# Latent value products with high and low values side by side

## The chip, the cores and the metric

The kernel runs on one core of one Trainium2 chip. The metric is the device time in microseconds, the median of several runs. TensorE is called PE in the profile, VectorE is DVE, ScalarE is ACT, GpSimd is POOL, and SP is the engine that issues most transfers.

## The reference, cut to what matters

One encoder layer on 768 tokens (a prompt of 512 and a sample of 256): a layer norm, a combined projection, two kinds of attention in parallel (latent attention with 8 heads, differential attention with 4), an output projection, a second norm, and 16 experts of which each token uses two. All in f32. The part at hand is the latent attention:

```
def mla_attention(q_nope, q_rope, k_nope, k_rope, v):
    scale = (MLA_NOPE_DIM + MLA_ROPE_DIM) ** -0.5
    ...
        s = (einsum('bqhd,bkhd->bhqk', qn, k_nope) + einsum('bqhr,bkr->bhqk', qr, k_rope))
        p = softmax(s * scale, axis=-1)
        return einsum('bhqk,bkhd->bqhd', p, v)
```

A head has 64 value columns. The differential heads add the bias -slope x |q - k| to their scores; the slope of head h is 0.25 to the power h + 1, and the table in memory holds -|q - k|.

## The kernel before, in words

**Splitting.** Every f32 operand x of a matmul is kept as two tiles, high (x copied into the type fp32r by ScalarE, names in `_h`) and low (x minus high, by VectorE or GpSimd, names in `_l`). A product is three matmuls: high x high, low x high, high x low; `three` makes the list and `products` (L647) issues it.

**The latent stage** runs as 48 slots s = 6h + i (8 heads, 6 query tiles of 128 each: four of the prompt with 512 keys, two of the sample with 256). Each engine goes through its own `mla_slot(s)` in order, and semaphores join them. In slot s:
- PE turns the probabilities of tile s (`turn_probs`, L782, into bank 2 or 3), computes pieces of block projections B (the differential q and k), the scores of tile s+4, at i = 4, 5 the value product of the head's prompt unit w = 2h, at i = 1 that of the last head's sample unit w = 2h-1, and at the end of a slot fills for the head two further on: K at i = 2, 3, Q at i = 4, 5, values V at `V_SLOTS`.
- ACT copies the turned probabilities (`probs_high`), takes exp of tile s+3, and copies fills (`high`). DVE does maximum, reciprocal, `probs_low`, `low`. POOL scales the probabilities of tile s+2 (`normalise`) and makes low parts of q and weights.

**Banks.** Fills go through banks 4 and 5 (`bank_order`), several in turn: bank 5 takes K, K, Q, Q, B of a head. `begin(g)` makes PE wait until the one before was copied high and low (or, for Q, multiplied into `q_raw` by `q_rotated`). In the slots the copies of a fill stand one slot after it.

**The value product.** `product(w)` has a stationary operand of 128 value columns, two heads side by side, of which the 64 rows of its own head are used, and the turned probabilities moving (512 or 256 columns). It accumulates in bank 6. `mix_high` copies the 64 rows to `mixM_h` and `mix_low` makes `mixM_l` from the bank and that copy; the next unit's product waits for `mix_low` (`m_ml`).

**The hand-over.** From s = 45 the slots z = s - 49 of the differential stage run along: `diff_scores(z+4)` on PE, `diff_biased(z+3)` on DVE (score plus bias table, and its maximum), `diff_exp(z+3)` on ACT in two halves, `diff_reciprocals(z+2)`, `diff_second(z+2)` on POOL, `diff_probs(z+1)` on DVE, `diff_turn_probs(z)` (L854) on PE, and the output of z-1 with `dpT_h`, `dpT_l`. Output projection pieces (`o_part`) begin at z = 3 and need four weight tiles split by `wo_high` on ACT (at z = -2 to 1) and `wo_low` on DVE (z = -1 to 2). The bias table is multiplied by 0.25 ahead of each head, by the first too (L1497). The first two `diff_output` wait for all of `mixM_l`.

Behind it come the output projection, router and experts; the experts' weights are fetched by transfers that wait for the router's results and for buffers.

Of the kernel before, what the change touches and what calls it, by code (L numbers as in the profile page):

```python
# [27 lines left out]
P = 128  # L28
# [32 lines left out]
def encoder_trunk(nc, x_prompt, x_sample, ln0_g, ln0_b, w_in, g_q, g_kv, w_uq, w_ukv, lam_q1, lam_k1,  # L61
# [88 lines left out]
    v_h = [at(f"v_h{i}", (132, 18)[i], [P, NT, 4 * VDIM], FR) for i in range(2)]  # L150
    v_l = [at(f"v_l{i}", (144, 24)[i], [P, NT, 4 * VDIM], FR) for i in range(2)]
# [4 lines left out]
    mixM_h = at("mixM_h", 126, [P, HEADS // 2, TOK], FR)  # L156
    mixM_l = at("mixM_l", 138, [P, HEADS // 2, TOK], FR)
# [168 lines left out]
    def filled(g):  # L326
# [4 lines left out]
        if g[0] == "V":  # L331
            vs = slice(2 * g[2], 2 * g[2] + 2)
            return bank[:].rearrange("p (t n) -> p t n", t=2), v_h[g[1]][:, vs, :], v_l[g[1]][:, vs, :]
# [37 lines left out]
    for k in range(0, 4, 2):  # L371
        z = 3 + 3 * (k // 2)
        O_EARLY[z], O_LATE[z], O_ADDS_FIRST[z + 1] = ((k, 0, 6),), ((k, 6, 12),), k
        O_LATE[z + 1], O_EARLY[z + 2], O_ADDS_LAST[z + 2] = ((k + 1, 0, 6),), ((k + 1, 6, 12),), k + 1
    WO_SLOTS = {15: 0, 16: 1, 17: 2, 21: 3}
# [134 lines left out]
    def mix_parts(n, c):  # L510
        return ((mixM_h, mixM_l), (mixD_h, mixD_l))[n][0][:, c, :], ((mixM_h, mixM_l), (mixD_h, mixD_l))[n][1][:, c, :]
# [120 lines left out]
    def front_pe(pe):  # L632
# [152 lines left out]
        def product(w, js):  # L785
# [3 lines left out]
            if js[0] == 0:  # L789
# [4 lines left out]
                wait(pe, m_ml, w)  # L794
            vs = slice((h % 4) // 2 * P, (h % 4) // 2 * P + P)
            pairs = three([(v_h[h // 4][:, t, vs], v_l[h // 4][:, t, vs], pT_h[x][:, j, :], pT_l[x][:, j, :])
                           for j, t in enumerate(range(SEQS[x][0] // P, SEQS[x][0] // P + nk))])

            last = products(psum[6][:, 0:n], pairs, 3 * js[0], 3 * js[-1] + 3)
# [9 lines left out]
        def mla_slot(s):  # L809
# [8 lines left out]
            if i == 1 and h:  # L818
                product(2 * h - 1, (0, 1))
# [37 lines left out]
        def diff_output(g):  # L857
# [5 lines left out]
            if g < 2:  # L863
                pe.wait_ge(m_ml, 2 * HEADS)
                pe.wait_ge(m_ptl, MT)
# [8 lines left out]
        def o_part(k, first, end):  # L874
# [4 lines left out]
            if first == 0:  # L879
                if n == 0:  # L880
                    pe.wait_ge(m_ml, 2 * HEADS if t >= NT_P else 2 * HEADS - 1)
# [98 lines left out]
    def front_act(act):  # L980
# [93 lines left out]

        def mix_high(w):
# [3 lines left out]
            act.wait_ge(m_pv, w + 1)  # L1079
            nc.scalar.activation(mixM_h[r, h // 2, t0:t0 + n], psum[6][r, 0:n], ACT.Copy).then_inc(m_mh, 1)  # L1080
# [10 lines left out]
        def mla_slot(s):  # L1091
            h, i = s // NT, s % NT
            if s < MT:
                probs_high(s)
            if i == 0 and h:
                mix_high(2 * h - 2)
            if i == 2 and h:
                mix_high(2 * h - 1)
            if s + 3 < MT:
                exp(s + 3)  # L1100
            if s >= MT:
# [1424 lines left out]
```

## Time and profile before

| | us |
|---|---|
| median of 3 runs | 803.47 (803.02 to 804.69) |
| the profiled execution, its time | 802.8 |
| its span, first to last instruction | 801.0 |
| PE busy in the span | 739.7 |
| mean granted TensorE clock | 0.98 of full |

The profile gives for each engine the time in which it was busy, the waits with what ended them, and a timeline with the start and duration of each instruction. Matmuls overlap: the duration of one is longer than the distance to the next, so their cost is read from the distances between starts. The granted clock is 1.00 at 2.4 GHz and 0.50 at 1.2 GHz. The latent slots run from about 110 to 276 us, the differential stage to about 390 us, the experts from about 455 us.

### The profile page before, as it was taken

What the parts mean: (1) busy time and instruction counts of PE and PEld (TensorE: products, weight loads), DVE (VectorE), ACT (ScalarE), POOL (GpSimd) and SP (SyncE); (2) the same over time, 40 slices, a digit from 0 to 9 for tenths busy, and PEclk for the clock granted to TensorE, in tenths of its full rate; (3) what the DMA queues carried; (4) which work ended last, traced back from release to release, by engine and by line L of the source; (5) the groups of instructions that cost most, each with busy time, mean ns of one, the idle gap of its engine ahead of it and who ended that gap; (6) DMA issues with size and microseconds to landing.
All of it is one profiled execution on the core that took longest, in us unless ns stands there. A gap on an engine that the chain in (4) does not pass through costs nothing.

```text
span 801.0 us, 12711 instructions
## 1 busy us (share of the span) xinstructions
PE 739.7 (92%) x3844; PEld 609.6 (76%) x3844; DVE 584.3 (73%) x975; ACT 482.5 (60%) x874; POOL 269.2 (34%) x292
## 2 busy tenths in 40 slices
PE   3999989998899889999999799999999999999985
PEld 3898878777778667777789577888877777777862
DVE  6964354555555586777678879999988888888857
ACT  3334355545554565667125447888788788888635
POOL 3132356545655243234421114222223222322111
PEclk9999999999999959999999999999999999999998
DMA  9724320222025492132645759999999999999863
GB/s 344 247 97 132 118 74 7 80 66 66 0 68 182 159 367 84 35 119 79 220 180 208 261 165 363 390 380 388 392 383 375 378 373 365 391 378 377 298 210 158
DMA packets 71485, 179.37 MB, mean 224 GB/s; under 512 B 11687, under 2 KB 28071, under 8 KB 71444
## 3 DMA queue, kind: packets, MB, share of 16 engines
q1 hardware_dynamic: 66692, 166.34, 55.2%
q0 software_dynamic: 4752, 12.51, 6.2%
q8 instruction: 23, 0.38, 0.2%
q14 instruction: 18, 0.15, 0.1%
HBM read 153.20 MB, written 30.42 MB: 229 GB/s over the span
## 4 chain that ended last, share of the span: by engine, by line
PE 55%; DMA 19%; DVE 14%; ACT 6%; issue 4%; POOL 1%; SPq 1%; ACTq 0%; DVEq 0%; POOLq 0%
PE bank L647 31%; DMA rawG<-in_w_gate 16%; PE bank L1767 4%; PE bank L1769 3%; PE bank L1768 3%; PE bank L782 2%; DVE eGl L1922 2%; DMA dv_l<-dv_low 2%; PE bank L1790 1%; PE bank L1789 1%; PE bank L1788 1%; ACT eGh L1852 1%; DVE eUl L1922 1%; PE bank L2147 1%; DVE eDl L1922 1%
## 5 line engine op out<-in xcount | busy, mean ns | idle before, releaser
L1922 DVE TENSOR_TENSOR eDl<-rawD,eDh 128x1024 fp32r<-128x1024 f32 x68 | 80.2, 1221 | 12.4 <-ACT eDh L1852 12.2
L1266 POOL TENSOR_SCALAR me<-me,mrec 128x512 f32<-128x512 f32 (+1 forms) x48 | 64.9, 1355 | 55.5 <-DVE mrec L1445 55.5
L1922 DVE TENSOR_TENSOR eGl<-rawG,eGh 128x1024 fp32r<-128x1024 f32 x64 | 75.5, 1222 | 7.5 <-ACT eGh L1852 6.6
L1922 DVE TENSOR_TENSOR eUl<-rawU,eUh 128x1024 fp32r<-128x1024 f32 x68 | 78.8, 1220 | 2.5 <-ACT eUh L1852 2.5
L2045 POOL DMA_INDIRECT acc_rows<-yg,idx_s x16 | 29.7, 1859 | 134.6 <-ACT yg L1877 134.6
L1852 ACT ACTIVATE eGh<-rawG 128x1024 fp32r<-128x1024 f32 x64 | 65.7, 1058 | 7.7 <-DMA rawG<-in_w_gate 7.2
L1072 ACT ACTIVATE pT_h<-bank 128x512 fp32r<-128x512 f32 (+1 forms) x48 | 25.3, 527 | 73.9 <-PE bank L782 73.9
L1451 DVE TENSOR_TENSOR pT_l<-bank,pT_h 128x512 fp32r<-128x512 f32 (+1 forms) x48 | 28.9, 602 | 50.3 <-ACT pT_h L1072 50.3
L1767 PE MATMUL bank<-eGh,xgT_h 128*128 128x512 f32 x136 | 56.5, 416 | 8.6 <-DVE xgT_l L1927 7.5
L1852 ACT ACTIVATE eDh<-rawD 128x1024 fp32r<-128x1024 f32 x64 | 64.0, 1055 | 0.0
L1852 ACT ACTIVATE eUh<-rawU 128x1024 fp32r<-128x1024 f32 x64 | 62.8, 1052 | 0.0
L1767 PE MATMUL bank<-eUh,xgT_h 128*128 128x512 f32 x136 | 54.6, 401 | 0.0
L1769 PE MATMUL bank<-eGl,xgT_h 128*128 128x512 f32 x136 | 53.8, 396 | 0.0
L1768 PE MATMUL bank<-eGh,xgT_l 128*128 128x512 f32 x136 | 53.4, 393 | 0.0
L1769 PE MATMUL bank<-eUl,xgT_h 128*128 128x512 f32 x136 | 53.2, 391 | 0.0
L1768 PE MATMUL bank<-eUh,xgT_l 128*128 128x512 f32 x136 | 52.9, 389 | 0.0
L1790 PE MATMUL bank<-eDl,hT_h 128*128 128x512 f32 x128 | 49.9, 390 | 0.0
L1788 PE MATMUL bank<-eDh,hT_h 128*128 128x512 f32 x128 | 49.8, 389 | 0.0
L1789 PE MATMUL bank<-eDh,hT_l 128*128 128x512 f32 x128 | 49.8, 389 | 0.0
L647 PE MATMUL bank<-xT_h,wb_h 128*128 128x256 f32 (+1 forms) x128 | 44.9, 351 | 4.0 <-DVE q_raw L1432 2.4
L647 PE MATMUL bank<-xT_h,wb_l 128*128 128x256 f32 (+1 forms) x128 | 43.7, 342 | 0.0
L647 PE MATMUL bank<-xT_l,wb_h 128*128 128x256 f32 (+1 forms) x128 | 43.7, 341 | 0.0
(345 smaller groups left out, 2171.6 us busy)
## 6 DMA issues: line engine op xcount, KB each, us to landing
rawG<-in_w_gate SPq DMA_DIRECT2D x68, 512.0 KB, 15.6
rawU<-in_w_up SPq DMA_DIRECT2D x68, 512.0 KB, 12.3
rawD<-in_w_down SPq DMA_DIRECT2D x68, 512.0 KB, 13.6
wb_raw<-in_w_in SPq DMA_DIRECT2D x8, 512.0 KB, 4.5
wo_raw<-in_w_o SPq DMA_DIRECT2D x8, 512.0 KB, 7.4
xln_rows<-res SPq DMA_DIRECT2D x6, 512.0 KB, 3.9
dqk_high<-st_h SPq DMA_DIRECT2D x8, 384.0 KB, 2.3
dqk_low<-st_l SPq DMA_DIRECT2D x8, 384.0 KB, 3.3
```

The source lines that it names most:

```text
L647: last = nc.tensor.matmul(out, pairs[i][0], pairs[i][1], start=(i == 0), stop=(i == n - 1))
L1266: nc.gpsimd.tensor_scalar(e, e, mrec[:, g % NSB:g % NSB + 1], None, ALU.mult).then_inc(m_p, 1)
L1451: nc.vector.tensor_tensor(pT_l[x][:, :, qs], psum[2 + g % 2][:, 0:n].rearrange("p (j q) -> p j q", q=P), f32(pT_h[x][:, :, qs]), ALU.subtr ...
L1767: nc.tensor.matmul(out, xgT_h[:, c, :], wh_[X][i][:, cs], start=(c == 0), stop=False)
L1768: nc.tensor.matmul(out, xgT_l[:, c, :], wh_[X][i][:, cs], start=False, stop=False)
L1769: last = nc.tensor.matmul(out, xgT_h[:, c, :], wl_[X][i][:, cs], start=False, stop=(c == KD - 1))
L1788: nc.tensor.matmul(out, hT_h[:, cs], wh_["D"][c][:, ns], start=(c == 0), stop=False)
L1789: nc.tensor.matmul(out, hT_l[:, cs], wh_["D"][c][:, ns], start=False, stop=False)
L1790: last = nc.tensor.matmul(out, hT_h[:, cs], wl_["D"][c][:, ns], start=False, stop=(c == 3))
L1852: nc.scalar.activation(wh_[X][i][:], raw_of(X, t, i)[:], ACT.Copy).then_inc(s_hi[X], 1)
L1922: nc.vector.tensor_tensor(wl_[X][i][:], raw_of(X, t, i)[:], f32(wh_[X][i][:]), ALU.subtract).then_inc(s_lo[X], 1)
L2045: pool.indirect_dma_start(out=acc_rows, out_offset=bass.IndirectOffsetOnAxis(ap=idx_s[:, 0:1], axis=0), in_=yg[:], in_offset=None, bounds_ ...
```

## The change

- The values are stored per head as 128 columns, 64 high and 64 low (`v_hl`). A product is now two matmuls per key tile, that stationary operand with the high and with the low probabilities; the rows of the bank hold the high values' part in one half and the low values' part in the other.
- The two halves are summed: ACT copies one half across partitions to `mixM_sum` (`mix_moved`), DVE adds the other (`mix_summed`), and then `mix_high` and `mix_low` split the sum, both operands now in SBUF. The next product waits for the sum alone. The order of these in each engine's slots is new.
- The copies of filled banks stand in the slot of the fill: B at i = 0, 1, K at 2, 3, V at its slot; `q_rotated(h+1, 1)` is ahead of `probs_low`.
- The hand-over: the last product moves from slot 49 to 48, `mix_moved(14)` to slot 47, the first reciprocals and probabilities of the differential stage and the wo copies to other slots (`WO_FIRST`), and the bias table comes multiplied by 0.25, so the first head's multiply is dropped.

```
```diff
@@ -147,14 +147,14 @@
     st_l = at("st_l", 121, [P, TOK], FR)
-    v_h = [at(f"v_h{i}", (132, 18)[i], [P, NT, 4 * VDIM], FR) for i in range(2)]
-    v_l = [at(f"v_l{i}", (144, 24)[i], [P, NT, 4 * VDIM], FR) for i in range(2)]
+    v_hl = [at(f"v_hl{i}", (138, 18)[i], [P, NT, 4, 2 * VDIM], FR) for i in range(2)]
...
     me = [at(f"me{i}", 198 + 2 * i, [P, 512]) for i in range(NME)]
-    mixM_h = at("mixM_h", 126, [P, HEADS // 2, TOK], FR)
-    mixM_l = at("mixM_l", 138, [P, HEADS // 2, TOK], FR)
+    mixM_h = [at(f"mixM_h{c}", 126 + 12 * (c // 2) + 3 * (c % 2), [P, TOK], FR) for c in range(HEADS // 2)]
+    mixM_sum = [at(f"mixM_sum{c}", 132 + 12 * (c // 2) + 3 * (c % 2), [P, TOK]) for c in range(HEADS // 2)]
+    mixM_l = [at(f"mixM_l{c}", 132 + 12 * (c // 2) + 3 * (c % 2), [P, TOK], FR) for c in range(HEADS // 2)]
@@ -330,7 +330,8 @@
             vs = slice(2 * g[2], 2 * g[2] + 2)
-            return bank[:].rearrange("p (t n) -> p t n", t=2), v_h[g[1]][:, vs, :], v_l[g[1]][:, vs, :]
+            v = v_hl[g[1]][:, vs, :, :]
+            return bank[:].rearrange("p (t h n) -> p t h n", t=2, h=4), v[:, :, :, 0:VDIM], v[:, :, :, VDIM:2 * VDIM]
@@ -372,6 +373,7 @@
         O_LATE[z + 1], O_EARLY[z + 2], O_ADDS_LAST[z + 2] = ((k + 1, 0, 6),), ((k + 1, 6, 12),), k + 1
+    WO_FIRST = {-1: (0,), 0: (1,), 1: (2, 3)}
@@ -508,7 +510,7 @@
     def mix_parts(n, c):
-        return ((mixM_h, mixM_l), (mixD_h, mixD_l))[n][0][:, c, :], ((mixM_h, mixM_l), (mixD_h, mixD_l))[n][1][:, c, :]
+        return (mixM_h[c][:], mixM_l[c][:]) if n == 0 else (mixD_h[:, c, :], mixD_l[:, c, :])
...
     def front_sync(sp):
         def load_x(t):
@@ -791,12 +793,13 @@
-                wait(pe, m_ml, w)
-            vs = slice((h % 4) // 2 * P, (h % 4) // 2 * P + P)
-            pairs = three([(v_h[h // 4][:, t, vs], v_l[h // 4][:, t, vs], pT_h[x][:, j, :], pT_l[x][:, j, :])
-                           for j, t in enumerate(range(SEQS[x][0] // P, SEQS[x][0] // P + nk))])
-            last = products(psum[6][:, 0:n], pairs, 3 * js[0], 3 * js[-1] + 3)
+                wait(pe, m_ml, 2 * w - 1)
+            pairs = []
+            for j, t in enumerate(range(SEQS[x][0] // P, SEQS[x][0] // P + nk)):
+                v = v_hl[h // 4][:, t, h % 4, :]
+                pairs += [(v, pT_h[x][:, j, :]), (v, pT_l[x][:, j, :])]
+            last = products(psum[6][:, 0:n], pairs, 2 * js[0], 2 * js[-1] + 2)
@@ -815,7 +818,7 @@
                 product(2 * h, ((0, 1), (2, 3))[i - 4])
-            if i == 1 and h:
+            if i == (1 if s < MT else 0) and h:
@@ -861,7 +864,7 @@
             if g < 2:
-                pe.wait_ge(m_ml, 2 * HEADS)
+                pe.wait_ge(m_ml, 4 * HEADS)
@@ -878,7 +881,7 @@
                 if n == 0:
-                    pe.wait_ge(m_ml, 2 * HEADS if t >= NT_P else 2 * HEADS - 1)
+                    pe.wait_ge(m_ml, 4 * HEADS if t >= NT_P else 4 * HEADS - 2)
@@ -1072,12 +1075,19 @@
+        def mix_moved(w):
+            h, x = w // 2, w % 2
+            t0, n, _ = SEQS[x]
+            r, other = (slice(VDIM * i, VDIM * i + VDIM) for i in (h % 2, 1 - h % 2))
+            act.wait_ge(m_pv, w + 1)
+            nc.scalar.activation(mixM_sum[h // 2][r, t0:t0 + n], psum[6][other, 0:n], ACT.Copy).then_inc(m_mh, 1)
         def mix_high(w):
...
             r = slice(VDIM * (h % 2), VDIM * (h % 2) + VDIM)
-            act.wait_ge(m_pv, w + 1)
-            nc.scalar.activation(mixM_h[r, h // 2, t0:t0 + n], psum[6][r, 0:n], ACT.Copy).then_inc(m_mh, 1)
+            act.wait_ge(m_ml, 2 * w + 1)
+            nc.scalar.activation(mixM_h[h // 2][r, t0:t0 + n], mixM_sum[h // 2][r, t0:t0 + n], ACT.Copy).then_inc(m_mh, 1)
...
         def wo_high(n, c):
@@ -1090,26 +1100,31 @@
         def mla_slot(s):
             h, i = s // NT, s % NT
+            if s > MT:
+                return
...
                 probs_high(s)
-            if i == 0 and h:
-                mix_high(2 * h - 2)
-            if i == 2 and h:
-                mix_high(2 * h - 1)
+            w = {0: 2 * h - 2, 2: 2 * h - 1}.get(i, -1) if s < MT - 1 else {MT - 1: 2 * HEADS - 2, MT: 2 * HEADS - 1}[s]
+            if s == MT:
+                mix_high(2 * HEADS - 2)
+            if w >= 0:
+                mix_moved(w)
...
                 exp(s + 3)
+            if 0 <= w < 2 * HEADS - 2:
+                mix_high(w)
...
                 q_high(h + 1, 1)
-            if i in (1, 2) and h - 1 in BLOCK_OF:
-                high(("B", BLOCK_OF[h - 1], i - 1))
-            if i in (3, 4) and h + 2 < HEADS:
-                high(("K", h + 2, i - 3))
+            if i in (0, 1) and h - 1 in BLOCK_OF:
+                high(("B", BLOCK_OF[h - 1], i))
+            if s in V_SLOTS:
+                high(("V", 1, V_SLOTS[s]))
+            if i in (2, 3) and h + 2 < HEADS:
+                high(("K", h + 2, i - 2))
...
                 q_high(h + 2, 0)
-            if s - 1 in V_SLOTS:
-                high(("V", 1, V_SLOTS[s - 1]))
@@ -1159,8 +1174,10 @@
                 diff_exp(z + 3, 1)
-            if -2 <= z < 2:
-                wo_high(0, z + 2)
+            if z == -1:
+                mix_high(2 * HEADS - 1)
+            for c in WO_FIRST.get(z, ()):
+                wo_high(0, c)
@@ -1451,13 +1468,21 @@
+        def mix_summed(w):
+            h, x = w // 2, w % 2
+            t0, n, _ = SEQS[x]
+            r = slice(VDIM * (h % 2), VDIM * (h % 2) + VDIM)
+            total = mixM_sum[h // 2][r, t0:t0 + n]
+            dve.wait_ge(m_mh, 2 * w + 1)
+            nc.vector.tensor_tensor(total, total, psum[6][r, 0:n], ALU.add).then_inc(m_ml, 1)
         def mix_low(w):
...
             r = slice(VDIM * (h % 2), VDIM * (h % 2) + VDIM)
-            dve.wait_ge(m_mh, w + 1)
-            nc.vector.tensor_tensor(mixM_l[r, h // 2, t0:t0 + n], psum[6][r, 0:n], f32(mixM_h[r, h // 2, t0:t0 + n]),
-                                    ALU.subtract).then_inc(m_ml, 1)
+            dve.wait_ge(m_mh, 2 * w + 2)
+            nc.vector.tensor_tensor(mixM_l[h // 2][r, t0:t0 + n], mixM_sum[h // 2][r, t0:t0 + n],
+                                    f32(mixM_h[h // 2][r, t0:t0 + n]), ALU.subtract).then_inc(m_ml, 1)
...
         def mla_slot(s):
@@ -1467,22 +1492,29 @@
                 q_rotated(h + 2, 0)
+            if i == 0 and 1 <= h < HEADS - 1:
+                q_rotated(h + 1, 1)
...
                 probs_low(s)
-            if i == 0 and h:
-                mix_low(2 * h - 2)
-            if i == 2 and h:
-                mix_low(2 * h - 1)
+            if s == MT - 1:
+                diff_reciprocals(0)
+            w = {0: 2 * h - 2, 2: 2 * h - 1}.get(i, -1) if s < MT - 1 else {MT - 1: 2 * HEADS - 2, MT: 2 * HEADS - 1}.get(s, -1)
+            if s == MT:
+                mix_low(2 * HEADS - 2)
+            if w >= 0:
+                mix_summed(w)
+            if s < MT and i in (1, 3) and h:
+                mix_low(2 * h - 2 + i // 2)
+            if s == MT + 1:
+                mix_low(2 * HEADS - 1)
...
                 return
-            if i == 0 and 1 <= h < HEADS - 1:
-                q_rotated(h + 1, 1)
-            if i in (1, 2) and h - 1 in BLOCK_OF:
-                low(("B", BLOCK_OF[h - 1], i - 1))
-            if i in (3, 4) and h + 2 < HEADS:
-                low(("K", h + 2, i - 3))
-            if s - 1 in V_SLOTS:
-                low(("V", 1, V_SLOTS[s - 1]))
+            if i in (0, 1) and h - 1 in BLOCK_OF:
+                low(("B", BLOCK_OF[h - 1], i))
+            if s in V_SLOTS:
+                low(("V", 1, V_SLOTS[s]))
+            if i in (2, 3) and h + 2 < HEADS:
+                low(("K", h + 2, i - 2))
...
         def wo_low(n, c):
@@ -1493,9 +1525,10 @@
                     dve.wait_ge(s_const, CONSTS + 16)
-                wait(dve, s_bias, 2 * g)
-                nc.vector.tensor_scalar_mul(bias_t[:], bias_t[:], 0.25).then_inc(s_in, 1)
-                dve.wait_ge(s_in, h + 1)
+                else:
+                    dve.wait_ge(s_bias, 2 * g)
+                    nc.vector.tensor_scalar_mul(bias_t[:], bias_t[:], 0.25).then_inc(s_in, 1)
+                    dve.wait_ge(s_in, h)
@@ -1544,18 +1577,21 @@
                 diff_mix_low(z - 3)
+            if z == -1:
+                diff_reciprocals(1)
+                diff_probs(0)
...
                 diff_biased(z + 3)
-            if 0 <= z + 1 < DT:
+            if 0 <= z and z + 1 < DT:
...
                 diff_probs_low(z)
-            if 0 <= z + 2 < DT:
+            if 0 <= z and z + 2 < DT:
...
                 o_first(O_ADDS_LAST[z])
-            if -1 <= z < 3:
-                wo_low(0, z + 1)
+            for c in WO_FIRST.get(z - 1, ()):
+                wo_low(0, c)
@@ -2486,7 +2522,7 @@
     rope_table = np.stack([np.concatenate([plain, turned]), np.concatenate([turned, plain])]).astype(np.float32)
-    dist = -np.abs(np.arange(P)[:, None] - (np.arange(ALIBI_W)[None, :] - (SEQ_P - P))).astype(np.float32)
+    dist = -0.25 * np.abs(np.arange(P)[:, None] - (np.arange(ALIBI_W)[None, :] - (SEQ_P - P))).astype(np.float32)
```

## Rows read from the trace of the kernel before

**Rows 1.** The page's busy table: us, share of the span, instructions.
```profile
PE 739.7 (92%) x3844; PEld 609.6 (76%) x3844; DVE 584.3 (73%) x975; ACT 482.5 (60%) x874; POOL 269.2 (34%) x292
```

**Rows 2.** Windows of 10 us: busy per engine, then granted clock, DMA share, GB/s.
```profile
150.00:160.00 10.00, 9.37 (x61) 8.32 (x60) 4.73 (x10) 5.51 (x13) 8.18 (x6) 1.00 0.09 29
...
190.00:200.00 10.00, 9.57 (x45) 8.06 (x46) 5.07 (x12) 4.82 (x11) 6.58 (x4) 0.83 0.12 37
...
280.00:290.00 10.00, 6.92 (x35) 5.54 (x35) 9.94 (x24) 8.88 (x20) 4.34 (x3) 0.51 1.03 366
290.00:300.00 10.00, 10.00 (x53) 8.53 (x53) 6.60 (x18) 5.05 (x17) 3.74 (x7) 0.64 0.94 380
```

**Rows 3.** The chain that ended last, by line, as the page has it.
```profile
PE bank L647 31%; DMA rawG<-in_w_gate 16%; PE bank L1767 4%; PE bank L1769 3%; PE bank L1768 3%; PE bank L782 2%; DVE eGl L1922 2%; DMA dv_l<-dv_low 2%; PE bank L1790 1%; PE bank L1789 1%; PE bank L1788 1%; ACT eGh L1852 1%; DVE eUl L1922 1%; PE bank L2147 1%; DVE eDl L1922 1%
```

**Rows 4.** Timeline of PE, value products of 512 and 256 columns: start, duration.
```profile
151.67 0.40 PE L647 MATMUL bank<-pT_h,v_l 128*128 128x512 f32 x1
151.90 0.39 PE L647 MATMUL bank<-pT_l,v_h 128*128 128x512 f32 x1
...
158.70 0.28 PE L647 MATMUL bank<-pT_h,v_l 128*128 128x256 f32 x1
158.82 0.28 PE L647 MATMUL bank<-pT_l,v_h 128*128 128x256 f32 x1
```

**Rows 5.** Waits in 105 to 400 us, PE's: total us, times, longest.
```profile
PE bank L647 <- DVE mixM_l L1459: 2.7, 2, 2.4
PE bank L647 <- DVE k_l L1422: 2.6, 3, 2.1
...
PE bank L647 <- DVE q_raw L1432: 2.4, 5, 0.6
...
PE bank L647 <- DVE v_l L1422: 1.6, 1, 1.6
...
PE bank L647 <- DVE st_l L1420: 0.8, 1, 0.8
```

**Rows 6.** Timeline of PE behind the wait for k_l that ended at 190.43.
```profile
192.05 0.63 PE L647 MATMUL bank<-pT_h,v_h 128*128 128x512 f32 x1
192.48 0.63 PE L647 MATMUL bank<-pT_h,v_l 128*128 128x512 f32 x1
```

**Rows 7.** Groups by form, 105 to 300 us: busy us, mean ns, idle before.
```profile
L1504 DVE CUSTOM_DVE_ANT_0 ee<-bank,bias_t 128x512 f32<-128x512 f32 x10 | 6.5, 688 | 0.1
L1459 DVE TENSOR_TENSOR mixM_l<-bank,mixM_h 64x512 fp32r<-64x512 f32 x8 | 5.5, 683 | 2.6 <-ACT mixM_h L1080 2.5
...
L1121 ACT ACTIVATE ee<-ee,negmax 128x512 f32<-128x512 f32 x10 | 7.1, 715 | 5.0 <-DVE negmax L1504 5.0
L1080 ACT ACTIVATE mixM_h<-bank 64x512 fp32r<-64x512 f32 x8 | 4.7, 588 | 0.1
```

**Rows 8.** Timeline of the hand-over, PE, then ACT.
```profile
274.54 0.40 PE L647 MATMUL bank<-pT_l,v_h 128*128 128x512 f32 x1
...
279.54 0.36 PE L647 MATMUL bank<-pT_h,v_h 128*128 128x256 f32 x1 [2.36 <-DVE mixM_l L1459]
...
281.46 1.12 PE L854 MATMUL bank<-ident,pp 128*128 128x128 f32 x4 [0.84 <-DVE pp L1517]
...
285.23 1.08 PE L854 MATMUL bank<-ident,pp 128*128 128x128 f32 x4 [1.72 <-DVE dpT_l L1523]
286.84 0.45 PE L647 MATMUL bank<-dv_h,dpT_h 128*128 128x128 f32 x1 [0.52 <-issue]
...
277.01 1.04 ACT L1089 ACTIVATE wo_h<-wo_raw 128x1024 fp32r<-128x1024 f32 x1
278.08 0.59 ACT L1080 ACTIVATE mixM_h<-bank 64x512 fp32r<-64x512 f32 x1
```

**Rows 9.** Timeline of POOL, `diff_second` beside an idle and a busy DVE.
```profile
276.35 0.78 POOL L1287 TENSOR_SCALAR ee<-ee,erec,lam_col 128x512 f32<-128x512 f32 x1 [5.46 <-DVE erec L1510]
281.58 1.66 POOL L1287 TENSOR_SCALAR ee<-ee,erec,lam_col 128x512 f32<-128x512 f32 x1 [4.46 <-DVE erec L1510]
```

## The prediction

> **What bounds the kernel now.** I read the page's busy table first: TensorE is busy 92% of the span and no other engine comes near [rows 1]. That is an average over stages, so next the windows of 10 us. In the latent-attention stage (110 to 270 us) a typical window has PE at 9.4 of 10 us with VectorE at 4.7, ScalarE at 5.5 and hardly any DMA [rows 2]. The chain of the page names the matmuls of `products` (L647) first and the gate-weight transfer second [rows 3]. The transfers of the experts are issued behind events that the front produces (logits, stored rows, low parts), so the expert stage moves as one piece when the front ends sooner; I found no transfer that runs on a date of its own. What is saved in the front is therefore saved at the end. The change touches only the latent stage and the hand-over to the differential heads, so all below is read there.
>
> **Part 1, two products for three.** `product` issued 3 matmuls per key tile, 12 of 512 columns and 6 of 256 columns per head; now 8 and 4. Removed in 8 heads: 32 of 512 columns and 16 of 256. What one costs is the distance between starts, not the duration (0.39 and 0.28 us, overlapped): 151.90 - 151.67 = 0.23 us and 158.82 - 158.70 = 0.12 us [rows 4]. 32 x 0.23 + 16 x 0.12 = 7.4 + 1.9 = 9.3 us. TensorE sets the pace there, so this lies on the path, but for what the hand-over takes back (part 4).
>
> The Trainium skill (TensorE: Matmul & The Clock Gate, Back-to-back issue gap) gives about 131 ns per matmul for a sustained stream of load and matmul pairs at 512 columns; by it the 32 long ones would be worth 4.2 us instead of 7.4, and the forecast would be 3 us later. The trace has 0.23 us for just such pairs [rows 4], and I go by the trace.
>
> **Part 2, the added copies.** Each of 16 units gets `mix_moved` on ScalarE and `mix_summed` on VectorE. The nearest rows are the old `mixM_h` (0.59 us for 64x512) and `mixM_l` (0.68) [rows 7]; with the 256-column halves at about two thirds, that adds some 8 us to each engine over 160 us. Those engines are half idle [rows 2], so the busy time is hidden under the matmuls. What matters is bank 6, which the next unit's first product waits for: before, high then low; now moved then summed, the same two operations. `mix_high` and `mix_low` come later, from SBUF. `mix_high(w)` stands behind `exp(s+3)` (0.7 us and its accumulator read), which covers the sum it waits for. Queued behind it are `q_high(h+1,1)`, then POOL's `q_low`; I put them where they are now. Bounds: 0 if covered, 16 x 0.6 = 10 us if every copy sat on the path; I take 0, since the idle time of both engines is nearest.
>
> One row gives pause: `diff_second`, an SBUF operation of POOL, took 0.78 us while VectorE was idle and 1.66 us while it ran operations with two SBUF inputs [rows 9]. `mix_low` now reads two SBUF tiles where it read a bank. At worst VectorE or POOL is held about 0.9 us in each of 16 slots; POOL works two slots ahead, so I count nothing, and keep this for the rival below. The Trainium skill (SBUF — State Buffer, SBUF: two separate sides) says that a VectorE operation with two SBUF inputs and a GpSimd one that reads SBUF exclude each other for a whole instruction; the two rows agree. By it and the 0.9 us of the rows, 16 low parts that each stood on the path would take 14 us back and leave the time near 801, which is rival D by another way.
>
> **Part 3, fills copied in their own slot.** `high`/`low` of B go from slots 1, 2 to 0, 1, of K from 3, 4 to 2, 3, of V one slot sooner; `q_rotated(h+1,1)` goes ahead of `probs_low`. They free the banks for which TensorE stood. The waits of PE there [rows 5], each with 0.15 us for the refilled pipeline:
> - q_raw, 5 times, 2.4 + 0.8 = 3.2 us. The block piece at the end of slot 0 waits for it; now it is issued before `probs_low`, held only by POOL's `q_low`, which ends a microsecond before PE arrives. Gone.
> - k_l, 3 times, 2.6 + 0.5 = 3.1 us, gone. The longest, 2.1 us, was followed by a fall of the clock: 192.48 - 192.05 = 0.43 us a matmul where 0.23 is usual [rows 6], and the window shows 0.83 [rows 2]. Seven matmuls x 0.2 = 1.4 us, gone too.
> - v_l, 1.6 + 0.15; the chain still has two copies, so I count half, 0.8 us.
> - st_l (L1420), 0.8 + 0.15 us, gone; its sister L1422 waits mostly ahead of the slots, and I count 0.2 of it: 1.2 us together.
> - mixM_l, 2.7 in two: 2.4 belongs to the hand-over, 0.3 stays.
> Sum 3.2 + 3.1 + 1.4 + 0.8 + 1.2 = 9.7 us. But ScalarE now stands at the end of a slot for the fill, in order, ahead of `probs_high` of the next slot, and slots are 1.2 us a head shorter; a K fill is followed at once by K's second half in the same bank. I take 2 us for new waits: net 8. Ends: 0 (every wait forms again elsewhere) and 10.
>
> **Part 4, the hand-over.** I went through the four queues by hand on the clock of the trace of before, with the durations of [rows 7]: a half of exp 0.72 and some 0.2 for the read of its sum, a half of biased 0.69 less a small overlap, copies and low parts 0.59 and 0.68. Before, TensorE stood until 279.54 for `mix_low(14)`, because `wo_high` at 277.01 was ahead of `mix_high(14)` at 278.08 on ScalarE; `diff_turn_probs` ran at 281.46 and 285.23 [rows 8]. Now `product(14)`, last issued at 274.54, is over 0.9 us sooner; moved 273.9 to 274.5, summed to 275.2, `product(15)` at 275.3, its stall of 2.4 us gone. The bias multiply, which stood ahead of the first biased scores, is gone too and lets the first exp start some 0.6 us sooner. But what is late next: `biased(1)` comes behind the sum (to 276.3), exp(1) to 277.6, `mix_high(14)` to 278.1, and VectorE's `mix_low(14)` waits for that with `mix_summed(15)`, `diff_reciprocals(1)` and `diff_probs(0)` queued behind it. `diff_turn_probs(0)` comes to 280.0, so PE is idle some 2.6 us from 277.3; `mix_high(15)` behind exp(2) ends 282.7, and the second turn comes to 285.6. From there PE is the bound at a halved clock: the windows 280 to 300 show 0.51 and 0.64 [rows 2]. First output about 286.5 by my schedule, 286.84 before: 0.35 us sooner, of the 0.9 that two products had saved. So the hand-over gains nothing and costs 0.6 us of part 1. Bounds: +3 us (one more gap like the one I drew) if `mix_high` runs a slot later, and -7 if the gap closes and the clock holds: the two windows hold 2 x (0.49 + 0.36) x 10 = 17 us at half clock, with PE 0.85 busy, and half of that is 7. Moving the wo copies later is covered by TensorE's own work at half clock: they are needed at z = 3 only. Without that cover one more wo copy, about as long as two copies of [rows 7], would be late.
>
> **Sum.** -9.3 + 0.6 - 8.0 = -16.7. Against the profiled execution: 802.8 us (span 801.0 and 1.8 around it) gives 786; against the median 803.5, 787. The two differ by 0.1%; I use the median.
>
> **Rivals.**
> - A, as above: 787 (782 to 792). Chance 0.55.
> - B, only the matmuls: the freed banks come sooner, but ScalarE's ordered waits and the two-input copies make as many new stalls. For: ScalarE waits for PE at nearly every slot; against: 9.4 of 10 busy already, and each stall of part 3 has one named cause. 803.5 - 9.3 + 0.6 = 795 (792 to 799). Chance 0.20.
> - C, the hand-over clears as well (the mechanism of its lower bound): 787 - 7 = 780. For: the half clock came after stalls at 279 to 285. Against: my schedule has as long a gap. Chance 0.12.
> - D, no change: the 8 us added to ScalarE and VectorE lie on the path and take back what the matmuls give: 803.5 - 9.3 + 8 = 802 (it would show as PE waits on the new copies). Against: half idle engines. Chance 0.05.
> - E, slower: the gap after 277.3 drops the clock and the loose start of the differential heads (turns at 280.0 and 285.6 waiting for copies) keeps it down. A microsecond of full PE at half clock costs half a microsecond, so it has to stay down 2 x 16.7 = 33 us longer than the 17 us of before to undo the gain; 40 us longer gives 806.5. Against: before, it was back inside the second window. Chance 0.08.
> The range goes from C into B: 778 to 798. A measurement of this kernel tells about 0.2% (1.6 us) from no change. Faster: A, B, C and some of D, 0.88; same 0.04; slower 0.08.
>
> **What the changed profile would show.** Products at the same 0.23 and 0.12 us, 64 of 512 and 32 of 256 columns. PE's waits for q_raw, k_l, st_l in 120 to 260 us near nothing, and the granted clock 1.00 at 185 to 200. In the hand-over, PE waiting for pp (behind mixM_l) for 2 to 3 us instead of for mixM_l, the clock low for some 17 us after it, and the first output about 16 to 17 us earlier than 286.84, near 270. After 300 us each stage as long as before. I am wrong if new waits on ScalarE's copies stand in PE's list with more than 3 us, or if the hand-over differs by more than 3 us from my schedule.

## The result, and the profile after

The changed kernel takes 797.86 us (median of 4 runs, 796.42 to 800.24) against 803.96 (803.02 to 804.69) for the kernel before on the same chip: 6.1 us less, ratio 0.9923, 95% interval 0.9897 to 0.9948. I had forecast 787. The sign was right, the size was not. The profiled execution has a span of 798.4 us, 2.6 under the 801.0 of before. The ratios here and below leave out executions in a slower state of the chip and are estimated from the single runs, so that they differ by up to 0.4% from the quotient of two medians.

**The matmuls did go away.** The timeline of PE in the changed kernel shows the value products at the distances forecast, two of each key tile, next to [rows 4]: 150.45 - 150.22 = 0.23 us and 157.02 - 156.91 = 0.11 us.

```profile
150.22 0.39 PE L649 MATMUL bank<-pT_h,v_hl 128*128 128x512 f32 x1
150.45 0.40 PE L649 MATMUL bank<-pT_l,v_hl 128*128 128x512 f32 x1
...
156.91 0.28 PE L649 MATMUL bank<-pT_h,v_hl 128*128 128x256 f32 x1
157.02 0.28 PE L649 MATMUL bank<-pT_l,v_hl 128*128 128x256 f32 x1
```

**The waits went only in part.** PE's waits in 100 to 300 us of the changed kernel (us in total, times, longest), to be read beside [rows 5]:

```profile
PE bank L857 <- DVE dpT_l L1556: 3.5, 1, 3.5
PE bank L649 <- DVE mixM_sum L1477: 2.8, 2, 2.2
PE bank L857 <- DVE pp L1550: 2.7, 1, 2.7
PE bank L784 <- POOL me L1283: 2.5, 2, 2.1
PE bank L649 <- DVE q_raw L1449: 2.3, 4, 0.6
PE bank L844 <- issue: 1.3, 1, 1.3
PE bank L649 <- DVE k_l L1439: 1.0, 1, 1.0
PE bank L649 <- DVE st_l L1439: 0.8, 1, 0.8
```

k_l fell from 2.6 to 1.0 us, v_l from 1.6 to 0.2, and the two rows of st_l (1.0 and 0.8 us before) to one of 0.8. But q_raw, forecast as gone, has 2.3 us in 4 against 2.4 in 5, and there is a new wait of 2.2 us for `mixM_sum`. DVE's own list of waits in 100 to 270 us names what holds q_raw; in the kernel before this row does not exist:

```profile
DVE q_raw L1449 <- POOL q_l L1264: 17.8, 6, 3.4
```

The place of the new wait, in the timelines of DVE, POOL and PE (start, duration; in brackets the idle time before and what ended it):

```profile
190.81 0.15 DVE L1462 RECIPROCAL mrec<-msum 128x1 f32<-128x1 f32 x1
194.31 0.43 DVE L1449 TENSOR_TENSOR q_raw<-bank,rope_t 128x256 f32<-128x256 f32 x1 [3.35 <-POOL q_l L1264]
194.65 0.68 DVE L1468 TENSOR_TENSOR pT_l<-bank,pT_h 128x512 fp32r<-128x512 f32 x1
195.37 0.69 DVE L1477 TENSOR_TENSOR mixM_sum<-mixM_sum,bank 64x512 f32<-64x512 f32 x1
...
189.01 2.40 POOL L1264 TENSOR_TENSOR wb_l<-wb_raw,wb_h 128x1024 fp32r<-128x1024 f32 x1 [0.47 <-ACT wb_h L1051]
191.40 1.57 POOL L1283 TENSOR_SCALAR me<-me,mrec 128x512 f32<-128x512 f32 x1
192.93 1.28 POOL L1264 TENSOR_TENSOR q_l<-q_raw,q_h 128x512 fp32r<-128x512 f32 x1
...
196.20 0.55 PE L649 MATMUL bank<-pT_h,v_hl 128*128 128x256 f32 x1 [2.17 <-DVE mixM_sum L1477]
```

There is one tile `q_raw`. `q_rotated(h+1, 1)` on DVE, in the first slot of head h, may write it only when POOL's `q_low(h+1, 0)` has read it, which POOL does at the end of the slot before. POOL works in order: the low part of the block weights, 2.40 us, then `normalise`, 1.57, then `q_low`, 1.28, which ends at 194.21. DVE stands at `q_rotated` for 3.35 us, and now `probs_low` and the mix's sum stand behind it. Before, `probs_low` was ahead of it and DVE's slack hid POOL's lateness. PE stands for 2.17 us until the sum is there, and behind that the granted clock falls: the windows of 10 us (busy per engine, then the granted clock) show 0.78 and 0.88, where [rows 2] had 0.83 and the window after it was 1.00. The low clock of the hand-over is as before:

```profile
190.00:200.00 10.00, 7.21 (x40) 6.06 (x39) 4.97 (x11) 5.87 (x15) 7.62 (x6) 0.78 0.01 2
200.00:210.00 10.00, 10.00 (x45) 8.12 (x44) 6.14 (x16) 5.31 (x13) 3.80 (x4) 0.88 0.00 0
270.00:280.00 10.00, 5.41 (x26) 4.74 (x26) 8.52 (x23) 7.98 (x18) 2.88 (x3) 0.53 1.04 382
280.00:290.00 10.00, 10.00 (x52) 8.47 (x51) 8.29 (x18) 5.95 (x18) 5.72 (x6) 0.61 0.89 364
```

**The hand-over** went as drawn. PE in the changed kernel, beside [rows 8]:

```profile
270.84 1.11 PE L857 MATMUL bank<-ident,pp 128*128 128x128 f32 x4 [2.66 <-DVE pp L1550]
...
276.72 1.09 PE L857 MATMUL bank<-ident,pp 128*128 128x128 f32 x4 [3.53 <-DVE dpT_l L1556]
```

### The profile page after: what moved, and what is told of

It is laid out like the page before. It is cut to its first block, busy times and chain, and to the rows that moved or that the text cites. A ratio compares the mean times of both kernels' runs of the same rounds, so it can differ in the third digit from the quotient of the medians.

```text
span 798.4 us, 12646 instructions
## 1 busy us (share of the span) xinstructions
PE 737.6 (92%) x3796; PEld 611.2 (77%) x3796; DVE 589.5 (74%) x990; ACT 493.6 (62%) x890; POOL 266.7 (33%) x292
## 4 chain that ended last, share of the span: by engine, by line
PE 53%; DMA 18%; DVE 13%; ACT 5%; POOL 5%; issue 4%; SPq 1%; DVEq 0%; ACTq 0%; POOLq 0%
PE bank L649 29%; DMA rawG<-in_w_gate 16%; PE bank L1803 4%; PE bank L1805 3%; PE bank L1804 3%; DVE eGl L1958 2%; POOL wb_l L1264 2%; POOL me L1283 2%; PE bank L1826 1%; PE bank L1825 1%; PE bank L1824 1%; PE bank L784 1%; PE bank L2183 1%; DMA dv_l<-dv_low 1%; ACT eGh L1888 1%
## 5 line engine op out<-in xcount | busy, mean ns | idle before, releaser
L1283 POOL TENSOR_SCALAR me<-me,mrec 128x512 f32<-128x512 f32 (+1 forms) x48 | 65.0, 1357 | 49.9 <-DVE mrec L1462 49.8
L649 PE MATMUL bank<-xT_h,wb_h 128*128 128x256 f32 (+1 forms) x128 | 46.2, 361 | 2.4 <-DVE q_raw L1449 2.3
L1304 POOL TENSOR_SCALAR ee<-ee,erec,lam_col 128x512 f32<-128x512 f32 (+1 forms) x24 | 21.9, 913 | 69.1 <-DVE erec L1543 69.1
L649 PE MATMUL bank<-xT_h,wb_l 128*128 128x256 f32 (+1 forms) x128 | 44.7, 349 | 0.0
L649 PE MATMUL bank<-xT_l,wb_h 128*128 128x256 f32 (+1 forms) x128 | 44.6, 349 | 0.0
L1894 ACT ACTIVATE xgT_h<-bank 128x512 fp32r<-128x512 f32 x34 | 20.3, 596 | 37.4 <-PE bank L1805 26.3
## 6 DMA issues: line engine op xcount, KB each, us to landing
rawG<-in_w_gate SPq DMA_DIRECT2D x68, 512.0 KB, 15.3
rawU<-in_w_up SPq DMA_DIRECT2D x68, 512.0 KB, 12.0
rawD<-in_w_down SPq DMA_DIRECT2D x68, 512.0 KB, 13.3
wb_raw<-in_w_in SPq DMA_DIRECT2D x8, 512.0 KB, 4.6
wo_raw<-in_w_o SPq DMA_DIRECT2D x8, 512.0 KB, 7.5
xln_rows<-res SPq DMA_DIRECT2D x6, 512.0 KB, 3.9
```

Source lines behind the costliest of these rows:

```text
L649: last = nc.tensor.matmul(out, pairs[i][0], pairs[i][1], start=(i == 0), stop=(i == n - 1))
L1283: nc.gpsimd.tensor_scalar(e, e, mrec[:, g % NSB:g % NSB + 1], None, ALU.mult).then_inc(m_p, 1)
L1304: nc.gpsimd.tensor_scalar(e, e, erec[:, g % NEE, 1:2], lam_col[:], ALU.mult, ALU.mult).then_inc(s_e2, 1)
```

## Where the time is, by stage

Starts of the first probability turn of a slot, read from the timelines, in us; "head" is slot 30 to slot 36, "rest" is from the fourth differential turn (z = 3) to the end of the span.

| kernel | slot 30 | head | slot 42 | slot 47 | z = 3 | rest |
|---|---|---|---|---|---|---|
| before | 219.64 | 22.26 | 260.34 | 273.10 | 295.85 | 505.2 |
| changed | 212.91 | 20.28 | 250.49 | 263.11 | 286.48 | 512.0 |
| changed, repeated (e1) | 213.78 | 20.24 | 251.31 | 263.95 | 287.31 | 504.8 |
| third matmul in it (e2) | 214.91 | 20.68 | 253.15 | 267.95 | 291.79 | 507.2 |
| fills' part alone (e4) | 214.22 | 20.68 | 252.47 | 264.96 | 287.98 | 511.1 |
| weights later (e7) | 208.45 | 19.54 | 244.40 | 257.02 | 280.38 | 507.5 |
| second q_raw (e8) | 207.31 | 19.53 | 243.25 | 255.88 | 279.24 | 507.1 |
| third matmul in that (e12) | 211.97 | 20.69 | 250.22 | 265.04 | 288.86 | 507.0 |
| second q_raw, hand-over (e10) | 206.46 | 19.53 | 242.40 | 255.03 | 275.46 | 512.4 |

At slot 47 the changed kernel is 10.0 us ahead where 17 were forecast. So the shortfall arises in the latent slots. The rest spreads over 7.6 us in these profiles. There the profiled execution lost 6.8 of the 9.4 us that it was ahead at z = 3; the repeat did not.

## The experiments

Each group was run beside the kernel before once more. Theory: POOL's late `q_low`, through the one tile `q_raw`, sets the pace of the changed slots. Rivals: the matmuls are worth less than their spacing; the added copies cost what they save; the fills' part brings nothing.

**First group**, the kernel before at 806.48 us (803.31 to 809.82). e1 is the changed kernel once more.

> The changed kernel once more, for a second profile. In its first profile it was 10.0 us ahead of the kernel before at slot 47, 9.4 at the third tile of the differential stage, and only 2.6 at the end: 3 us went at a wait for dv_low with the clock at half behind it, 2.5 at half clock in the router, 1.5 at the end. Theory T (those are chance: where the clock falls differs from run to run): ahead by 9 to 10 at slot 47 again, but the later losses differ by a microsecond or more, and the median is 5 to 8 us under before. Rival R (the change causes them): the same losses at the same places.

797.73 us (792.71 to 800.34), ratio 0.9889 (0.9850 to 0.9928): 8.8 us, a little more than the 5 to 8 expected. Slot 47 is 9.2 us ahead, as expected.

e2, the changed kernel with a third matmul per key tile:

```diff
-                pairs += [(v, pT_h[x][:, j, :]), (v, pT_l[x][:, j, :])]
+                pairs += [(v, pT_h[x][:, j, :]), (v, pT_l[x][:, j, :]), (v, pT_l[x][:, j, :])]
```

> The changed kernel with a third matmul per key tile again (it adds the low probabilities twice, which changes the output a little). Theory T (each removed matmul is worth its 0.23 or 0.12 us, so 9.3 us were the matmuls and almost nothing the rest): 8 to 10 us slower than the changed kernel, so 1 to 3 us slower than before. Rival (the matmuls fill idle time that waits leave, and the 10 us at slot 47 come from the copies in their own slot): 2 to 5 us slower than the changed kernel.

801.09 us, ratio 0.9941 (0.9917 to 0.9966): 3.4 us over e1. In the head it takes 0.44 us more than e1, where four matmuls of 0.23 and two of 0.12 make 1.16; the saved matmuls were mostly waited away. At slot 42 it is 1.8 us behind e1, which understates it, since e1 began slot 0 0.9 us later and had the longer spell of low clock behind slot 25. The head has neither.

e3, `q_rotated(h+1, 1)` on DVE behind `probs_low` and the sum, as before:

```diff
-            if i == 0 and 1 <= h < HEADS - 1:
-                q_rotated(h + 1, 1)
             if s < MT:
                 probs_low(s)
...
+            if i == 0 and 1 <= h < HEADS - 1:
+                q_rotated(h + 1, 1)
```

> The changed kernel with q_rotated(h+1,1) back behind probs_low and the sum on VectorE. Theory T (VectorE stood 3.35 us for POOL's q_low there, and the sum behind it held the product of slot 25 for 2.2 us and the clock fell for 6.8): the wait for mixM_sum in slot 25 shrinks under 1 us, 2 to 4 us faster than the changed kernel at slot 28, the waits for q_raw at the end of slot 0 stay at 0.5 to 0.8. Rival (the order is neutral, the stall is the copies' own length): within 1 us of the changed kernel.

793.31 us, ratio 0.9826 (0.9785 to 0.9866). Undoing the step that I had credited with 3.2 us takes 4.4 us off the median of e1, though the two intervals just overlap. The trace is clearer: from slot 6 to slot 47 it takes 128.3 us against 131.5 in the changed kernel and in e1, so 3.2 us come off, free of the fall of the clock at 117 us that e3 happened not to have. The wait for the sum is gone from PE's list in 100 to 255 us and the clock of 190 to 210 us is full; q_raw's stays:

```profile
PE bank L784 <- POOL me L1283: 3.8, 3, 2.1
PE bank L649 <- DVE q_raw L1449: 2.6, 5, 0.6
```

It stays for another reason: DVE now waits for POOL's `q_low` only once (0.7 us), but `q_rotated` comes directly behind the sum, and the head is as long as before the edit (20.27). So the forward place seems to pay only if the tile is free by then; no run has the second tile with the old place.

e4, the kernel before with the fills' copies in their own slot and `q_rotated` ahead, nothing else (ACT's half; DVE's is the same):

```diff
-            if i in (1, 2) and h - 1 in BLOCK_OF:
-                high(("B", BLOCK_OF[h - 1], i - 1))
-            if i in (3, 4) and h + 2 < HEADS:
-                high(("K", h + 2, i - 3))
+            if i in (0, 1) and h - 1 in BLOCK_OF:
+                high(("B", BLOCK_OF[h - 1], i))
+            if s in V_SLOTS:
+                high(("V", 1, V_SLOTS[s]))
+            if i in (2, 3) and h + 2 < HEADS:
+                high(("K", h + 2, i - 2))
```

> The kernel before with only the copies of filled banks in their own slot and q_rotated ahead of probs_low. My prediction gave that part 8 us. Theory T (it moved waits rather than removed them): 0 to 3 us faster than before. Rival (it is worth what I gave it and the sum and its copies eat it in the changed kernel): 6 to 9 us faster.

797.32 us, ratio 0.9878 (0.9840 to 0.9916): 9.2 us, as much as the whole change, and the theory (0 to 3) fell. This part was forecast at 8. Of PE's waits in 100 to 300 us, q_raw is gone altogether and k_l nearly; the stall behind DVE's wait is there, 2.1 of the 4.5 us for `mixM_l`:

```profile
PE bank L647 <- DVE mixM_l L1459: 4.5, 2, 2.4
PE bank L647 <- DVE k_l L1422: 0.4, 1, 0.4
```

**Second group**, the kernel before at 806.54 us (803.25 to 811.06). e5 and e6 leave out the product of high values and low probabilities, in the kernel before and in e4:

```diff
+            pairs = [p for i, p in enumerate(pairs) if i % 3 < 2]
-            last = products(psum[6][:, 0:n], pairs, 3 * js[0], 3 * js[-1] + 3)
+            last = products(psum[6][:, 0:n], pairs, 2 * js[0], 2 * js[-1] + 2)
```

> The kernel before with two of the three matmuls per key tile (high values by low probabilities left out) and nothing else. It takes away the same 48 matmuls. Theory P (each slot train of TensorE ends in a wait for q_raw or k_l, set by POOL and by copies; what is taken from a slot with such a wait comes back as a longer wait): 3 to 6 us faster than before, and in the trace the waits for q_raw are longer by 0.4 to 0.5 each. Rival N (TensorE is the bound and all 9.3 us come out): 8 to 10 us faster.

> The kernel with only the copies of fills in their own slot, and two of three matmuls, with the old copies of the value product. Theory P (the lost part of the matmuls' worth is POOL's q_low behind the weights' low part, not the added copies): 2 to 5 us faster than with three, with waits for q_raw of 0.5 to 0.8 at slots 6, 12, 30, 36 and a stall at slots 25 to 26, as in the changed kernel. Rival C (the added mix_moved and mix_summed take it back): 8 to 9 us faster than with three and no such waits.

e5 800.83 us, ratio 0.9928 (0.9906 to 0.9950), 5.7 us; e6 792.27, 0.9831 (0.9790 to 0.9871), 14.3 us, 5.1 beyond e4. In e5 the size came as expected, the place did not: the waits for q_raw are still 2.4 us in 5, those for k_l grew from 2.6 us in 3 to 4.5 in 8. In e6 the wait for q_raw, which e4 did not have, is back:

```profile
PE bank L647 <- DVE q_raw L1433: 2.2, 4, 0.6
```

POOL's `q_low` and PE's next use of that bank, at slot 30, in e4 (three matmuls) and then in the changed kernel (two):

```profile
214.50 1.30 POOL L1247 TENSOR_TENSOR q_l<-q_raw,q_h 128x512 fp32r<-128x512 f32 x1
216.63 0.28 PE L647 MATMUL bank<-xT_h,wb_h 128*128 128x256 f32 x1
```

```profile
214.10 1.29 POOL L1264 TENSOR_TENSOR q_l<-q_raw,q_h 128x512 fp32r<-128x512 f32 x1
215.97 0.38 PE L649 MATMUL bank<-xT_h,wb_h 128*128 128x256 f32 x1 [0.50 <-DVE q_raw L1449]
```

With three matmuls `q_low` ends 0.8 us ahead of PE. With two, PE is there before `q_low` has ended.

The added copies do not slow the head: it is 20.24 in e6 and e1, and 20.68 in e4 and e2, with the old copies and with the new. But e6 reaches slot 47 3.6 us sooner than e1 (260.33). That difference has no clean cause: it holds a longer spell of low clock in e1 behind slot 25, and in e6 the old order of the hand-over.

e7, POOL's `block_weights_low` one place later, behind `q_low`:

```diff
-                if i == 4 and h in NEXT_BLOCK:
-                    block_weights_low(NEXT_BLOCK[h])
...
+                if i == 5 and h in NEXT_BLOCK:
+                    block_weights_low(NEXT_BLOCK[h])
```

e8, a second tile for the rotated queries of the sample:

```diff
-    q_raw = at("q_raw", 124, [P, SEQ_P])
+    q_raws = [at("q_raw", 124, [P, SEQ_P]), at("q_raw_s", 206, [P, SEQ_S])]
...
-            wait(dve, s_ql, nth_q[g])
+            wait(dve, s_ql, nth_q[g] - 1)
```

> The changed kernel with POOL's block_weights_low moved from i = 4 to i = 5, behind q_low. Theory P: the waits for q_raw at slots 6, 12, 30, 36 (0.5 to 0.63 each) go, the wait of VectorE for q_l in slot 24 falls from 3.35 us to under 1 and with it the stall for mixM_sum; slot 47 comes 4 to 8 us sooner than in the changed kernel. Rival C: slot 47 within 1 us.

> The changed kernel with a second q_raw tile for the sample tokens, so that q_rotated(h+1,1) needs no finished q_low. Theory P (the single q_raw tile is what ties VectorE to POOL): as the POOL order, slot 47 comes 4 to 8 us sooner than in the changed kernel and the q_raw waits go. Rival (POOL's length alone matters, through q_h and the scaled probabilities): slot 47 within 1 us.

e7 788.73 us, ratio 0.9771 (0.9732 to 0.9810); e8 787.77, 0.9781 (0.9734 to 0.9828): 17.8 and 18.8 us, twice the repeat's. Each undoes one link of the chain POOL, tile, DVE, PE, from different ends, and the head is the same, 19.54 and 19.53. Slot 47 comes 6.1 and 7.2 us sooner than in the changed kernel, within the 4 to 8 expected. In e7 DVE still waits for POOL, 7.1 us in 6 and at most 1.4, where I had expected under 1; PE waits 0.9 us for the sum once. In e8's list, 100 to 255 us, PE's waits for q_raw and for the sum are both gone; DVE's timeline at the same place has no wait for POOL; the sum starts at 191.34 us, 2.0 us behind the start of slot 24, instead of at 195.37, 4.5 behind it; and the clock of 190 to 200 us is full:

```profile
PE bank L784 <- POOL me L1283: 3.8, 3, 2.1
PE bank L844 <- issue: 1.3, 1, 1.3
PE bank L649 <- DVE k_l L1439: 1.0, 1, 1.0
PE bank L649 <- DVE st_l L1439: 0.8, 1, 0.8
PE bank L649 <- DVE pT_l L1468: 0.4, 1, 0.4
```

```profile
189.55 0.42 DVE L1449 TENSOR_TENSOR q_raw_s<-bank,rope_t 128x256 f32<-128x256 f32 x1
191.34 0.69 DVE L1477 TENSOR_TENSOR mixM_sum<-mixM_sum,bank 64x512 f32<-64x512 f32 x1
```

```profile
190.00:200.00 10.00, 8.25 (x49) 6.93 (x48) 6.51 (x13) 7.46 (x17) 7.37 (x6) 1.00 0.00 0
```

**Third group**, the kernel before at 805.03 us (803.04 to 809.64). e9 is the changed kernel with another order in the hand-over; e10 is e8 with it, e11 is e10 with the edit of e7 too. ACT, and `diff_probs(0)` on DVE likewise ahead of `mix_low(14)`:

```diff
-            if s == MT:
-                mix_high(2 * HEADS - 2)
             if w >= 0:
                 mix_moved(w)
...
-            if 0 <= w < 2 * HEADS - 2:
+            if w >= 0:
                 mix_high(w)
...
-            if z == -1:
-                mix_high(2 * HEADS - 1)
```

> The changed kernel with only the hand-over from prefill to the decoding blocks reordered: ScalarE copies the mix of slot 46 right behind its sum, ahead of exp(1), and the mix of slot 47 ahead of exp(2); VectorE makes the first difference products ahead of the low mix of slot 46. All of the computation stays. Theory (the hand-over's remaining waits, 2.65 us for pp and 3.53 us for dpT_l, are an order of the queues): the stretch from the start of slot 47 to the third difference product gets 1 to 3 us shorter, 23.4 to about 21, and the whole 1 to 3 us under the changed kernel repeated on its chip, 795 to 797 on that chip's scale. Rival (the hand-over is bound by TensorE at the half clock, so that a wait removed comes back as another): that stretch within 0.5 us of 23.4, the time within 1 us of the changed kernel's.

> The changed kernel with a second tile for the sample tokens' rotated queries and the reordered hand-over of the run before. All of the computation stays. Theory (the two gains lie in different places and add): slot 47 begins where it does with the second tile alone, 17 us sooner than in the kernel before, and the third difference product 18 to 20 us sooner; 1 to 3 us under the second tile alone, ratio 0.975 to 0.978. Rival (hand-over bound by TensorE at half clock): ratio 0.977 to 0.980, as with the second tile alone.

> As the run before, and GpSimd's step for the block weights' low part one place later too. All of the computation stays. Theory (both edits cure the same wait, GpSimd's late q_low holding the one tile): slot 47 begins within 1 us of the second tile alone, and the time is within 1.5 us of the run before. Rival (GpSimd's order costs something of its own, beyond the shared tile): another 2 us or more come off, slot 47 begins 19 us or more sooner than in the kernel before.

From slot 47 to z = 3 it takes 20.43 us in e9 and e10 and 20.44 in e11, 2.9 less than the 23.37 of the changed kernel: the theory held. The wait for pp is gone and the one for dpT_l is 2.55 us instead of 3.53, for a new one of 1.83 for negmax. PE's timeline in e10:

```profile
262.52 0.39 PE L844 MATMUL bank<-dk_h,dq_h 64*128 64x256 f32 x2 [1.83 <-DVE negmax L1534]
265.70 1.09 PE L857 MATMUL bank<-ident,pp 128*128 128x128 f32 x4 [2.55 <-DVE dpT_l L1553]
```

Times: e9 793.47, ratio 0.9856 (0.9815 to 0.9897); e10 786.67, 0.9735 (0.9700 to 0.9769); e11 785.03, 0.9764 (0.9732 to 0.9797). e10 and e11 are the fastest kernels of the study; the intervals of e10, e11, e7 and e8 overlap, so that the hand-over's 2.9 us show in the traces rather than in the ratios. The same holds of e9 beside e1. e11 has slot 47 1.2 us later than e10, and the same head: both edits cure one wait, as expected, and the rival (slot 47 at least 19 us sooner than before) fell at 16.8.

e12, e8 with the third matmul of e2:

> The kernel with the second tile for rotated queries, but with a third matmul in each key tile of the value products (low probabilities times the values a second time, so the output counts the low probabilities twice): 48 matmuls more, each about 0.23 us. In the changed kernel the same addition cost 3.4 us. Theory (GpSimd's queue held the slots there, so that TensorE's saved time went into waiting; with the tile doubled TensorE sets the slots): it costs 7 to 10 us here, slot 47 begins 7 to 10 us later than with the second tile alone, and the time is near 795 to 798. Rival (the matmuls are worth little anywhere, since they are covered by other engines in most slots): again 2 to 5 us, near 790 to 793.

797.14 us, ratio 0.9897 (0.9867 to 0.9928), where e8 has 0.9781: 0.0116 x 805 = 9.3 us. The traces tell it apart: 1.16 us in the head, 7.0 us at slot 42, 9.2 at slot 47, of which some 2 go to a low clock after 261 us that e8 did not have there (e2 has the same against e1, at 264). With one tile the same matmuls cost 0.44, 1.8 and 4.0. With three matmuls the head is 20.69 here and 20.68 in e2 and e4: there one tile or two makes no difference, since PE is the slowest.

## Why the prediction was right in sign and wrong in size

The step that failed is the first of part 3: "held only by POOL's `q_low`, which ends a microsecond before PE arrives. Gone." It failed in two ways.

- The microsecond was read at PE's pace of before, and then added to part 1, which brings PE to that place 1.16 us a head sooner; the prediction itself has "slots are 1.2 us a head shorter", but in the line on new waits. With three matmuls the step holds: in e4 and e2 PE's waits for q_raw are gone. With two they come back, 2.2 us in 4 in e6 and 2.3 in 4 in the changed kernel, and the head stays at 20.28 us where it is 19.53 with a second tile.
- DVE's arrival was not looked at. In its new place `q_rotated` comes to DVE some 3 us before `q_low` is done, and holds `probs_low` and the sum. I counted what frees PE and not what queues behind the moved instruction. That made the stall at slot 25 with the low clock behind it, 3.2 us up to slot 47 (e3).

Part by part:

- Part 1, the matmuls, forecast -9.3: the size per matmul was right, 1.16 us a head in e8 against e12, on the path only where POOL does not hold the slots. In the changed kernel a third matmul costs 0.44 us a head, and 3.4 us in all (e1 against e2). "This lies on the path" was true of the slots with the second tile and false of those with the change as made. By the 131 ns that the Trainium skill states (TensorE: Matmul & The Clock Gate, Back-to-back issue gap) the four long ones would be worth an estimated 4 x 0.131 = 0.5 us a head; the trace differs, with 0.23 us each, 0.9 for the four, and the measured 1.16 for all six decides.
- Part 2, the copies at nothing: right. With three matmuls, where PE sets the pace, the head is 20.68 with the old copies (e4) and with the new (e2). Nor did `mix_low` with two SBUF operands hold up the slots: with it in place the full 1.16 us came out.
- Part 3, forecast -8.0: right by itself, in e4, and not beside part 1. e4 is 9.2 us under before and 8.1 ahead at slot 47; q_raw gave all of its 2.4 us, k_l 2.2 of 2.6, v_l all of 1.6, st_l 1.0 of 1.8, and a new wait of 2.1 us stands against the 2 that I had set aside. In the changed kernel k_l gave 1.6 of 2.6 us, v_l 1.4 of 1.6, st_l the same 1.0, q_raw nothing. In both the clock fell again, behind the new wait, so that its 1.4 us did not come.
- The two parts did not add. Forecast -17.3 without the hand-over; 9.2 for the fills' part alone, 5.7 for two matmuls alone, together 8.8 by the repeat's median, the hand-over's 0.6 within it. With the wait on POOL taken out (e8), slot 47 is 17.2 us ahead of before: about the forecast, by an edit that the change lacks. That it fits so closely is in part luck, since a chance fall of the clock at 118 us took 1.6 us of it.
- Part 4, forecast +0.6: too small. Slot 47 to z = 3 is 22.75 us before and 23.37 after, but this +0.62 is not the forecast's 0.6, which was to be taken from what fewer matmuls save. Slot 42 to z = 3 has four long and four short ones fewer, worth 1.4 us, and went from 35.51 to 35.99: 1.9 us were taken back. e6, with two matmuls and the old hand-over, has 35.27 there, so that the new hand-over alone costs 0.7. My schedule was right in its gaps: the gap of 2.6 us ahead of the first turn was measured as 2.66, the turns stand 5.88 us apart where I had 5.6, and the clock shows 0.53 and 0.61. Rival C's price, 7 us, was too high: a better order gives 2.9.
- Rival B, 795 (792 to 799), named the outcome's size but not its cause: it put the new stalls on ACT's ordered waits and the two-input copies; they were DVE's wait on POOL. A, C, D and E fell.

Still open is a part of what the profiled execution of the changed kernel lost behind z = 3, 6.8 us. It waits 2.0 us for the transfer of `dv_l`, and the granted clock is 0.83 in the window 340 to 350 us. The wait is not chance: it is 0.8 us in two before, 1.7 us in e1 and 1.2 to 2.5 in all the kernels with two matmuls, whose fronts end sooner; the forecast had each stage after 300 us as long as before. The fall of the clock behind it is another matter: e1 has the wait and a clock of 1.00 there. So I hold the clock's share for the spread between executions, without having shown what starts it.

## What to carry to other kernels

When an instruction is moved forward in an in-order queue, compare the end of everything that it waits for with the time at which its own engine now reaches it, and count what stands behind it, before crediting the bank that it frees. A scratch tile that two engines hand back and forth is such a wait, and a second one (1 KB a partition here) was worth 7 to 8 us at slot 47, and 10 us between the savings of the two medians, 18.8 and 8.8. A margin read in the trace of before holds only at the pace of before: where one part of a change makes the engine come sooner, take that off the margin before the next part is added. Two savings measured alone at 9.2 and 5.7 us can give 9 together, where one of them uses up the margin that the other rests on; the stretch of one regular head, free of the clock's chance, shows this where medians do not.

## What the runs showed of the hardware

After one and the same wait the clock falls in one execution and not in another. In all 14 profiles PE waits some 2.1 us for POOL's `me` at about 117 us; in 7 the clock falls right after it and in 7 not. The kernels e1 and e3 have the same instructions up to there and ran on the same chip; it fell in e1, as in the changed kernel, and not in e3. PE's timeline of the changed kernel, then that of e3:

```profile
116.97 1.05 PE L784 MATMUL bank<-ident,me 128*128 128x128 f32 x4 [2.09 <-POOL me L1283]
```

```profile
116.92 0.66 PE L784 MATMUL bank<-ident,me 128*128 128x128 f32 x4 [2.06 <-POOL me L1283]
```

The four matmuls take 1.05 us in the one and 0.66 in the other, and the granted clock in 110 to 120 us is 0.85 and 1.00. One such fall costs 1.6 us here (slot 6 starts at +0.31 us in the changed kernel and at -1.34 in e3, against before, which had no fall there). Executions of one kernel can thus differ by such falls; the runs of one kernel in a group spread over 5 to 14 us, and I did not separate how much of that the falls make.
